# Pooled and turned products of the second mixer moved into dense tile slots between three projection blocks, with another order of the operand splits

## What is computed

```python
xn = rms_norm_2(h, g_mix_pre[i])
z = xn @ w_in[i]
conf_ab, q, k, v, f_logit, sc_h, sc_b, sc_c, pool_v = jnp.split(z, SPLIT_IDX, axis=-1)
y_conf = conformer_conv(conf_ab, ...)        # a*sigmoid(b), causal conv of 31 taps, layer norm, silu, @ w_pw
y_att = forgetting_attention(q, k, v, f_logit + b_forget[i])
y_sc = short_conv_mixer(sc_h, sc_b, sc_c, w_sc[i])     # sc_b * conv3(sc_c * sc_h)
y_pool = multiscale_pool(pool_v, w_pool[i], pool_scale[i])
mix = jnp.concatenate([y_conf, y_att, y_sc, y_pool], axis=-1) @ w_out[i]
h = h + rms_norm_2(mix, g_mix_post[i])
```

```python
def multiscale_pool(v, w_pool, scale):
    ...            # four groups of 64 columns: mean over the last 2, 4, 8, 16 tokens, minus the value
    d = jnp.stack(outs, axis=2).astype(v.dtype)
    d = jnp.einsum("bsgc,gcd->bsgd", d, w_pool).reshape(b, s, D_POOL)
    return d * scale
```

## Time and profile before

| | |
|---|---|
| three executions | 2834.41, 2836.91, 2838.14 us |
| profiled execution | 2837.19 us, span of its instructions 2835.2 us |
| busy in the span | PE 2659.4 us (94%), DVE 918.7, POOL 876.7, ACT 818.8 |
| mean granted clock of PE | 0.956 of full speed |
| E... blocks with the attention | 1568 to 1779 us of the span |
| Esc1, Esb1 with conf 0 to 4 | 1779 to 1818.4 us |
| mix, until x0 runs | 1818.4 to 1834.4 us |

### The profile page before, as it was taken

The page is one execution under the profiler, slowest core; times in us unless marked ns, Lnnn a source line. Parts: engine busy times, 40 slices in busy tenths (PEclk is TensorE's granted clock), DMA queues, the critical chain, the costliest instruction groups (busy, mean ns, idle before and its releaser), DMA issues.

```text
span 2835.2 us, 30314 instructions
## 1 busy us (share of the span) xinstructions
PE 2659.4 (94%) x12580; PEld 2120.9 (75%) x12580; DVE 918.7 (32%) x1435; ACT 818.8 (29%) x1219; POOL 876.7 (31%) x492
## 2 busy tenths in 40 slices
PE   7798999999997998999999899898999999999896
PEld 5677778666686777787777677687888888888785
DVE  5213430323203544411237557404022222222423
ACT  4103441344322444422232333223211111111321
POOL 2122112444322111134642121235333323333633
PEclk8899999999998999999989899999999999999898
DMA  7001101100011000011212000120111111111111
GB/s 292 31 29 37 38 25 48 34 19 19 15 52 53 10 19 12 14 47 43 100 41 98 23 23 15 39 101 23 52 52 45 45 52 45 52 52 45 51 38 69
DMA packets 34440, 134.84 MB, mean 48 GB/s; under 512 B 3648, under 2 KB 4096, under 8 KB 32896
## 3 DMA queue, kind: packets, MB, share of 16 engines
q1 hardware_dynamic: 33984, 131.85, 13.4%
q10 hardware_dynamic: 320, 1.05, 0.1%
HBM read 123.45 MB, written 8.39 MB: 47 GB/s over the span
## 4 chain that ended last, share of the span: by engine, by line
PE 88%; DVE 5%; ACT 3%; POOL 2%; issue 1%; DMA 0%; POOLq 0%; SPq 0%; ACTq 0%; DVEq 0%
PE slot L667 55%; PE slot L713 12%; PE ps L894 4%; PE ps L865 3%; PE ps L843 2%; PE ps L745 2%; PE ps L927 1%; PE ps L918 1%; PE ps L931 1%; PE ps L944 1%; DVE cacc L2103 1%; PE ps L788 1%; POOL wlo L1505 1%; PE ps L771 1%; ACT zs L1233 0%
## 5 line engine op out<-in xcount | busy, mean ns | idle before, releaser
L667 PE MATMUL slot<-xhi,whi 128*128 128x512 f32 x2192 | 715.2, 408 | 59.2 <-ACT zs L1233 16.8
L667 PE MATMUL slot<-xlo,whi 128*128 128x512 f32 x2192 | 691.9, 397 | 0.0
L667 PE MATMUL slot<-xhi,wlo 128*128 128x512 f32 x2192 | 687.7, 395 | 0.0
L1505 POOL TENSOR_TENSOR wlo<-raw,whi 128x1024 fp32r<-128x1024 f32 (+1 forms) x169 | 429.6, 2542 | 832.3 <-ACT whi L1141 832.3
L667 PEld LDWEIGHTS slot<-xhi,whi 128*128 128x128 f32 x2192 | 404.9, 193 | 147.9 <-issue 66.1
L667 PEld LDWEIGHTS slot<-xlo,whi 128*128 128x128 f32 x2192 | 421.6, 192 | 92.1
L667 PEld LDWEIGHTS slot<-xhi,wlo 128*128 128x128 f32 x2192 | 420.0, 192 | 92.1
L1141 ACT ACTIVATE whi<-raw 128x1024 fp32r<-128x1024 f32 (+1 forms) x169 | 186.1, 1101 | 332.9 <-PE slot L713 174.1
L713 PE MATMUL slot<-uhi,whi 128*128 128x512 f32 x512 | 158.3, 390 | 0.0
L713 PE MATMUL slot<-ulo,whi 128*128 128x512 f32 x512 | 157.7, 389 | 0.0
L713 PE MATMUL slot<-uhi,wlo 128*128 128x512 f32 x512 | 157.6, 389 | 0.0
(11 more groups left out here) (326 smaller groups left out, 3054.0 us busy)
## 6 DMA issues: line engine op xcount, KB each, us to landing
raw<-wstream SPq DMA_DIRECT2D x129, 512.0 KB, 3.2
raw<-wstream SPq DMA_DIRECT2D x40, 640.0 KB, 3.9
ada<-wada SPq DMA_DIRECT2D x7, 1024.0 KB, 19.9
mm<-xT SPq DMA_DIRECT2D x2, 2048.0 KB, 9.8
ada<-wada SPq DMA_DIRECT2D x2, 2048.0 KB, 27.1
mm<-xT SPq DMA_DIRECT2D x8, 512.0 KB, 4.5
res_dram<-mm SPq DMA_DIRECT2D x8, 512.0 KB, 3.0
res<-res_dram SPq DMA_DIRECT2D x8, 512.0 KB, 6.5
```

Source lines behind the costliest of these rows:

```text
L667: o = mm_(outs[:, half * HALF:(half + 1) * HALF], w[b % 2][:, k_w, :], x[:, k_x, half * HALF:(half + 1) * HALF], start=first and j == 0, s ...
L1505: tt(flat(wlo[b % 2])[:, 0:n], (raw1 if b == 1 else raw)[:, 0:n], flat(whi[b % 2])[:, 0:n].bitcast(F32), ALU.subtract).then_inc(w_lo, 1)
```

## The change

Three things are done.

1. The layer norm `conf` 0 and 1 are spread over `Esh1`, conf 2 over `Esc1`, conf 3 and 4 over `Esb1`. `Esh1` is taken out of the list over which the attention, the conv taps and the pool's sums are spread; these are spread over the blocks up to `Esb0` alone.
2. `mix` loses its PE work. The two turned tiles become events `yturn` 0 and 1 between `Esh1` and `Esc1`, the two pool products become `poolpw` 0 and 1 between `Esc1` and `Esb1`. All four are numbered tiles and take slots: yE0 138, yE1 139, Esc1 140, pool0 141, pool1 142, Esb1 143. The pool product is written as four 64x64 pieces a tile in place of one 128x128 matrix for two halves; its weights (128x128 floats in place of 128x256) go to a part of `tab` that is free by then, and their DMA is issued after those that save the residual, 14 weight blocks earlier in SP's queue.
3. The order of the splits becomes 6, 7, 2, 3, 4, 5, 0, 1 (pool, attention, short conv, conv) in place of 4, 5, 0, 1, 2, 3, 6, 7.

```diff
--- before.py
+++ after.py
@@ -257,7 +257,7 @@
 
-    proj = proj_events("E") + dense_part_events("E" + n for n in ("p0", "p1", "sh0", "sc0", "sb0", "sh1"))
+    proj = proj_events("E") + dense_part_events("E" + n for n in ("p0", "p1", "sh0", "sc0", "sb0"))
     taps = proj.index(("dense", INDEX["Eca1"], PARTS["F"] - 1)) + 1
...
@@ -271,8 +271,9 @@
     tl += spread(rest[:pooled], late[:ahead]) + spread(rest[pooled:], behind)
-    tl += spread(dense_part_events(["Esc1", "Esb1"])[:-2], [("conf", n) for n in range(5)])
-    tl += dense_part_events(["Esb1"])[-2:]
+    tl += spread(dense_part_events(["Esh1"]), [("conf", 0), ("conf", 1)]) + [("yturn", 0), ("yturn", 1)]
+    tl += spread(dense_part_events(["Esc1"]), [("conf", 2)]) + [("poolpw", 0), ("poolpw", 1)]
+    tl += spread(dense_part_events(["Esb1"])[:-2], [("conf", 3), ("conf", 4)]) + dense_part_events(["Esb1"])[-2:]
     tl += [("mix",)]
...
@@ -288,6 +289,7 @@
 TIMELINE = list_timeline()
+MIX_ORDER = (2, 3, 6, 7, 0, 1)
 
...
@@ -304,10 +306,9 @@
             g += 1
-        elif ev[0] == "mix":
-            tiles["yE0"] = g
-            g += 2
-    tiles["yE1"] = tiles["yE0"] + 1
+        elif ev[0] in ("yturn", "poolpw"):
+            tiles[("yE%d" if ev[0] == "yturn" else "pool%d") % ev[1]] = g
+            g += 1
     return tiles
...
@@ -548,6 +548,7 @@
         ct = tab[:, TABLES["strict"][0]:TABLES["strict"][0] + S]
+        wpls = tab[:, TABLES["dist"][0] - P:TABLES["dist"][0]].rearrange("p (t d) -> p t d", t=2)
         windows = (wsum, zs[0])
...
@@ -566,8 +567,8 @@
 
-        mix_sources = [(4, scy[:, 0, :]), (5, scy[:, 1, :]), (0, cu[:, 0, :]), (1, cu[:, 1, :]),
-                       (2, pbuf[0][:]), (3, pbuf[1][:]), (6, sx[:]), (7, su[:])]
+        mix_sources = [(6, sx[:]), (7, su[:]), (2, pbuf[0][:]), (3, pbuf[1][:]),
+                       (4, scy[:, 0, :]), (5, scy[:, 1, :]), (0, cu[:, 0, :]), (1, cu[:, 1, :])]
 
...
@@ -621,16 +622,16 @@
                         sp.dma_start(res_dram[:, n, :], mm[:, n, :]).then_inc(res_out, 16)
+                    sp.dma_start(wpls, wpool).then_inc(wpool_in, 16)
                 elif ev == ("conf", 0):
 
                     sp.wait_ge(s_norm, 128)
                     sp.dma_start(wpws[:], wpw).then_inc(pw_in, 16)
-                    sp.dma_start(wpls[:], wpool).then_inc(pw_in, 16)
                 elif ev[0] == "dense" and ev[2] == 3 and BLOCKS[ev[1]][1] == "x1":
                     sp.wait_ge(res_out, 16 * NC)
                     wait_tile(sp, TILE["yE1"])
                     wait_all_split(sp, 3)
-                    sp.wait_ge(m_pool, 2)
+                    sp.wait_ge(m_pw_in, 2)
                     for n in range(NC):
...
@@ -1103,7 +1104,7 @@
                     pe.wait_ge(m_silu, 2)
-                    pe.wait_ge(pw_in, 32)
+                    pe.wait_ge(pw_in, 16)
                     if n:
...
@@ -1111,21 +1112,20 @@
                     o.then_inc(m_pw, 1)
-                elif ev[0] == "mix":
-
+                elif ev[0] == "yturn":
                     pe.wait_ge(s_norm, 128)
-                    for n in range(2):
-                        ytrans(TILE["yE%d" % n], n)
-
-                    pe.wait_ge(m_pw_in, 2)
-                    for t in range(2):
-                        pe.wait_ge(pl_done, t + 1)
-                        if t:
-                            pe.wait_ge(m_pool_in, 1)
-                        for half in range(2):
-                            o = mm_(psb[half], wpls[:, t, :], (sx, su)[t][:, half * HALF:(half + 1) * HALF],
-                                    start=True, stop=True)
-                        o.then_inc(m_pool, 1)
+                    ytrans(TILE["yE%d" % ev[1]], ev[1])
+                elif ev[0] == "poolpw":
+
+                    t, g = ev[1], TILE["pool%d" % ev[1]]
+                    wait_slot(g)
+                    pe.wait_ge(wpool_in, 16)
+                    pe.wait_ge(pl_done, t + 1)
+                    for half in range(2):
+                        for r0 in (0, DH):
+                            o = mm_(slot[g % 2][r0:r0 + DH, half * HALF:(half + 1) * HALF], wpls[r0:r0 + DH, t, :],
+                                    (sx, su)[t][r0:r0 + DH, half * HALF:(half + 1) * HALF], start=True, stop=True)
+                    o.then_inc(tile_done, 1)
 
...
@@ -1475,10 +1475,11 @@
                     split_weights(INDEX["x1"])
-                    act.wait_ge(sc_done, 2)
                     for pos, (k, src) in enumerate(mix_sources):
-                        if pos >= 2:
-                            act.wait_ge(mix_src, pos - 1)
+                        if k in (4, 5):
+                            act.wait_ge(sc_done, k - 3)
+                        else:
+                            act.wait_ge(mix_src, MIX_ORDER.index(k) + 1)
                         split_wide(k, src)
...
@@ -2175,22 +2176,20 @@
                 elif ev[0] == "mix":
-                    split_wide(3, 0, 4, scy[:, 0, :])
-                    split_wide(3, 2, 0, cu[:, 0, :])
-                    for t in range(2):
-                        g = TILE["yE%d" % t]
-                        wait_tile(dve, g)
-                        v.tensor_copy(pbuf[t][:], slot[g % 2][:]).then_inc(slot_free[g % 2], 1)
-                        wait_evacuated(dve, "yE%d" % t)
-                        v.tensor_copy(token[:, 0:1], token[:, 1:2]).then_inc(mix_src, 1)
-                    split_wide(3, 4, 2, pbuf[0][:])
-                    for t in range(2):
-                        dve.wait_ge(m_pool, t + 1)
-                        v.tensor_scalar((sx, su)[t][:], ps4[:], v_("pool_scale", t, 1), None, ALU.mult
-                                        ).then_inc(m_pool_in, 1)
-                        dve.wait_ge(m_pool_in, t + 1)
-                        v.tensor_copy(token[:, 0:1], token[:, 1:2]).then_inc(mix_src, 1)
-                    split_wide(3, 6, 6, sx[:])
+                    for pos in range(0, NC, 2):
+                        split_wide(3, pos, *mix_sources[pos])
+                elif ev[0] in ("yturn", "poolpw"):
+                    name = ("yE%d" if ev[0] == "yturn" else "pool%d") % ev[1]
+                    g = TILE[name]
+                    wait_tile(dve, g)
+                    if ev[0] == "yturn":
+                        ins = v.tensor_copy(pbuf[ev[1]][:], slot[g % 2][:])
+                    else:
+                        ins = v.tensor_scalar((sx, su)[ev[1]][:], slot[g % 2][:], v_("pool_scale", ev[1], 1), None,
+                                              ALU.mult)
+                    ins.then_inc(slot_free[g % 2], 1)
+                    wait_evacuated(dve, name)
+                    v.tensor_copy(token[:, 0:1], token[:, 1:2]).then_inc(mix_src, 1)
                 elif ev == ("conf", 0):
...
@@ -2340,10 +2339,7 @@
     w1, w2 = inp["cmp_w1"][0], inp["cmp_w2"][0]
-    wp = np.zeros((P, 2, P), np.float32)
-    for g in range(4):
-        r = DH * (g % 2)
-        wp[r:r + DH, g // 2, r:r + DH] = inp["w_pool_2"][0, g]
+    wp = inp["w_pool_2"][0].reshape(2, 2, DH, DH).transpose(1, 2, 0, 3).reshape(P, 2, DH)
     arrays = {
         "xT": inp["x"][0].T.reshape(NC, P, S).transpose(1, 0, 2),
         "pT": inp["p_2"][0, 0].T.reshape(2, P, S).transpose(1, 0, 2),

```

More of the change, by code:

```diff
@@ L461, in build @@
         wpws = at("wpws", 161, [P, 2, BW])
-        wpls = at("wpls", 165, [P, 2, P])
         def t_(name, a=0, n=None):
@@ L512, in build @@
             sem("f_%s" % n) for n in ("x", "abs", "log", "c", "ct", "ci", "bc", "cb"))
-        conf_done, m_mean, m_cent, m_sq, m_var, m_std, m_hat, m_silu, m_pw, m_pool, m_pool_in, sc_done, pl_in, pl_done = (
+        conf_done, m_mean, m_cent, m_sq, m_var, m_std, m_hat, m_silu, m_pw, wpool_in, sc_done, pl_in, pl_done = (
             sem(n) for n in ("conf_done", "m_mean", "m_cent", "m_sq", "m_var", "m_std", "m_hat", "m_silu", "m_pw",
-                             "m_pool", "m_pool_in", "sc_done", "pl_in", "pl_done"))
+                             "wpool_in", "sc_done", "pl_in", "pl_done"))
         pe_order = sem("pe_order")
```

## The result

The changed kernel takes 2842.26 us, the median of 20 executions (2837.69 to 2850.73). The kernel before takes 2837.76 us beside it, also 20 executions (2834.24 to 2842.91). The ratio is 1.0019, with a 95% interval of 1.0012 to 1.0027: slower by about 4.5 us, a difference under 0.2% that the interval still sets apart from none. I had forecast 2841.5 us. The profiled execution took 2844.37 us, 7.2 us more than the profiled one before, so the two profiles differ by more than the medians do.

The account below looks back on a forecast made before the run. PE was taken as the bound, with 88% of the span, so only its holes and the slow clock behind them count. Terms -10.1 + 2.4 + 10.0 + 2.0 = +4.3 us on 2837.2 gave 2841.5 us, range 2832.5 to 2849.

Parts of the forecast that it names:

- Term A: From the end of Esb1 to x0 at full speed: only the splits are left, -10.1 us (-11.8 to -8.4).
- Term B: Between Esh1 and Esc1: the turned tiles now stand there, delaying Esc1 by +2.4 us (1.9 to 3.3).
- Term C: From T2 (PE ends Esc1) to Esb1: Esb1 waits for pool0's slot, +8.5 plus 1.5 slow clock, +10.0 us.
- The step on the pieces: Pool products before Esb1: 64-row pieces run side by side, so a tile costs 1.72 us as before.
- the rival with the pieces one after the other: Pool products: 64-row pieces don't overlap, 3.44 us a tile, Esb1 starts at the same time; 2840.0 us, chance 0.18.
- Term D: Attention stage: without Esh1's cover, holes open on PE, chiefly about 2 us near Esc0; +2.0 us (-3 to +7).
- Conf 1's slow stretch stays: Layer norm: the half-speed clock behind conf 1's one-column matmuls stays as before, with nothing added to the sum.
- DVE as the bound of the attention stage: Rival at Esc0 and Esb0: DVE becomes the bound, term D up to +7; 2845.5 us with D = 6, chance 0.30.
- The mix did get short: Denies the rival that the mix doesn't get short because x0 waits for something else; 2845 to 2848 us, chance 0.08.
- the holes cost what I had said: Holes behind Esc1 and Esb1, sized in terms C and A; the rival had them cheaper, 2831 us, faster by over 0.2%: 0.12.

Follow-up runs that it names:

- e1: Changed kernel, but DVE runs the short conv's taps of Esc1 only after scaling pool0 and pool1; 2835.24 us, 0.9993 to the kernel before.
- e4: Changed kernel, but POOL makes x0's low weights only after pool0's slot is read out; 2838.63 us, 1.0008 to the kernel before.
- e9: Changed kernel with only the pool-product pieces of rows 0 to 63, the others left out; 2840.38 us in one execution.
- e5: Changed kernel with the pool-product pieces of rows 0 to 63 first, then rows 64 to 127, not alternating; 2843.88 us, 1.0020 to the kernel before.
- e2b: Kernel before with only the new spread of attention and layer norm, the mix as before, run again for its trace; 2837.65 us in one execution.
- e7: e1 with ACT also splitting the first chunk before making x1's high weights; 2836.15 us, 0.9999 to the kernel before.

## Why the prediction was right, and where it was not

The total was right within 1 us, and that was partly luck. The terms that the sum has came to +1.9 us up to the norm, with conf 1 in it, where +4.3 were forecast; slow clock behind the region, for which the sum has no term, made up the difference. Terms A, B and C, the mechanism that the forecast rests on, were right.

- **Term A, the mix gets shorter: right.** Predicted -10.1, measured -10.2. PE stood idle for 4.83 us (4.9 said), ended by DVE's `xlo` of `sx`, with ACT and POOL in the order given, and the clock was 0.55 behind. The line by line count from the rows of the old mix held because the same three operations met in the same way.
- **Term B, the turned tiles: right.** +2.6 against +2.4.
- **Term C, the pool products: right in mechanism and size.** Predicted T2 + 8.5 and 1.5 us of slow clock; measured T2 + 8.3 and 1.7. e1 shows that the place in DVE's queue was the cause, e4 that POOL's turn was 2.1 us of the 2.4 that I had put there. The step on the pieces (1.72 us a tile, side by side) was right as well, with 1.93 us to the end of the last record. Hence the rival with the pieces one after the other falls. The Trainium skill, TensorEngine Tiling (Array Packing), Restrictions and Gotchas, says that different row tiles cannot access the same PSUM bank at a time; e9 and e5 disagree for two row tiles that write different partition halves of a bank, and the measurement decides.
- **Term D, the attention stage loses cover: wrong in sign.** Predicted +2.0, measured -1.9, inside its bounds of -3 to +7. The hole next to Esc0 did come. DVE was taken up by the pool step, the read-out with its taps and the conv tap from 1739.67 to 1748.77 us (8.8 us were forecast, though the rows named for it add up to 8.2), and PE waited for the `ytok` behind them. Before, it had waited at the same place too:

```profile
1736.24 0.41 PE L865 MATMUL ps<-brv,pbuf 128*128 128x64 f32 x2 [1.03 <-DVE ytok L1859]
...
1739.67 1.24 DVE L1804 SCALAR_TENSOR_TENSOR su<-wsum,tab,su 64x1008 f32<-64x1008 f32 x1
1748.77 0.28 DVE L1860 TENSOR_SCALAR ytok<-ps,fac 128x64 f32<-128x64 f32 x1
1749.20 1.30 PE L866 MATMUL ps<-brv,pbuf 128*128 128x64 f32 x10 [1.64 <-DVE ytok L1860]
```

  The steps that failed are two. The term took the whole hole as new, where 1.03 of its 1.64 us stood there before, so 0.6 and not 2.0 were added. And it left the wait on `brq` out of the middle value and had its end only in the lower bound: these 2.4 us went. The other waits of the stage changed by -0.1 together. e2b has the same -1.7, the same 1.64 us and no `brq` wait, so the new spread alone does both. Why the wait on `brq` goes was not looked into further.
- **"Conf 1's slow stretch stays": wrong.** It doubled, 6.8 us in place of 3.4, and cost +1.4 us. It did so in the trace of every kernel with the new spread but e7's, which had none there (1.00 from 1778.5 to 1800) and more slow clock in the attention stage (208.5 us to conf 0 in place of 201.1). What decides between one length and the other is open.
- **What I left out altogether** is what comes after the region: +1.0 us at the norm behind the `w_out` blocks, and up to +2.0 at the end of the program, in some executions. The region itself gives +1.9 us; the median says +4.5. What the profiles show of the difference is slow clock elsewhere. They show it moving from place to place, and don't settle how much of it the change causes.

Of the other rivals, DVE as the bound of the attention stage didn't come about (123.69 of 198.70 us busy, and PE's holes fewer). The mix did get short. In the changed kernel's traces the holes cost what I had said; in e1 the same hole in front of x0 cost more.

## What to carry to other kernels

A product that is moved into a tile slot costs what its read-out's place in the reader's queue makes of it: put the reads that free a slot ahead of work that frees none, as e1 did for 7.2 us between the medians. A hole that a dependence makes unavoidable can be filled with real work whose result is needed late, as conf 4 was; dummy work keeps the clock up, but gained nothing in the median here. A sum of a few microseconds over a whole program should carry a term for the slow clock that moves elsewhere, since within one kernel a change of 0.001 in the mean clock was worth 2 us.
